# Values' weight slabs in pairs with 512 moving columns, in a kernel of three transformer layers

## The reference

```python
h = _rmsnorm(x, g_mix[layer])
proj = jnp.einsum('bsd,de->bse', h, w_in[layer])
sb_q, sb_k, sb_v, da_q, da_k, da_v = jnp.split(proj, ...)      # 512 columns each
o_a = _stick_breaking_attention(heads(sb_q), heads(sb_k), heads(sb_v))
o_b = _diff_attention(q1, q2, k1, k2, heads(da_v), lam)        # q, k normed and rotated
...
proj = xn @ w_in                                                # second layer
q, k, v = proj[..., :1024], proj[..., 1024:2048], proj[..., 2048:3072]
log_f = jax.nn.log_sigmoid(proj[..., 3072:] + b_f)              # forgetting gates
o = causal_block_attention(q, k, v, 1.0 / math.sqrt(64), jnp.cumsum(log_f, axis=1))
```

## Time and profile before

| | us |
|---|---|
| median of 3 runs | 1010.24 |
| lowest, highest | 1009.67, 1011.06 |
| span of the profiled execution | 1007.6 |
| PE busy | 993.9 (99%) |
| DVE busy | 714.1 (71%) |
| ACT busy | 607.8 (60%) |

### The profile page before, as it was taken

The page is one execution under the profiler, slowest core; times in us unless marked ns, Lnnn a source line. Parts: engine busy times, 40 slices in busy tenths (PEclk is TensorE's granted clock), DMA queues, the critical chain, the costliest instruction groups (busy, mean ns, idle before and its releaser), DMA issues.

```text
span 1007.6 us, 19765 instructions
## 1 busy us (share of the span) xinstructions
PE 993.9 (99%) x7214; PEld 923.4 (92%) x7214; DVE 714.1 (71%) x1360; ACT 607.8 (60%) x1094; POOL 59.6 (6%) x79
## 2 busy tenths in 40 slices
PE   8999999999999999999999999999999999999997
PEld 8999989999999999989999999999989999999996
DVE  4668987776666668666496666668977686666665
ACT  5677785575555556565475555557768675555553
POOL 3011110120000002000020000002200010000000
PEclk9999999999999999999999999999999999999999
DMA  7743445466555554433545556564665456565631
GB/s 292 273 149 110 153 145 187 148 206 190 176 181 186 183 189 159 157 127 127 167 146 188 187 187 187 187 187 127 203 194 191 146 167 188 187 187 187 187 125 43
DMA packets 50904, 174.05 MB, mean 173 GB/s; under 512 B 6304, under 2 KB 8864, under 8 KB 50720
## 3 DMA queue, kind: packets, MB, share of 16 engines
q1 hardware_dynamic: 49664, 172.12, 52.9%
q10 hardware_dynamic: 1184, 1.18, 0.6%
HBM read 169.86 MB, written 1.05 MB: 170 GB/s over the span
## 4 chain that ended last, share of the span: by engine, by line
PE 90%; DVE 5%; ACT 2%; DMA 1%; issue 1%; SPq 0%; DVEq 0%; ACTq 0%
PE bank L426 89%; DVE w_lo L1485 2%; PE bank L647 1%; DVE a_pair L1504 1%; DMA stage<-slab_dram 1%; DVE xT L1515 1%; DVE arena L1478 0%; ACT w_hi L1032 0%; ACT a_pair L1067 0%; DVE soft_s L1566 0%; ACT soft_p L1124 0%; ACT w_hi L1016 0%; DVE tmp L1478 0%; DVE tmp L1712 0%; DVE arena_r L1485 0%
## 5 line engine op out<-in xcount | busy, mean ns | idle before, releaser
L426 PE MATMUL bank<-a_pair,w_hi 128*128 128x256 f32 (+1 forms) x1992 | 537.8, 342 | 2.8 <-DVE w_lo L1485 2.7
L426 PE MATMUL bank<-a_pair,w_lo 128*128 128x256 f32 x1488 | 417.6, 282 | 0.0
L1485 DVE TENSOR_TENSOR w_lo<-stage,w_hi 128x1024 fp32r<-128x1024 f32 (+2 forms) x322 | 387.4, 1211 | 8.4 <-ACT w_hi L1016 3.5
L426 PEld LDWEIGHTS bank<-a_pair,w_hi 128*128 128x128 f32 x1992 | 343.4, 190 | 48.6 <-DVE w_lo L1485 4.0
L426 PE MATMUL bank<-arena_r,w_hi 128*128 128x256 f32 x1792 | 328.8, 284 | 0.4 <-DVE arena_r L1485 0.2
L426 PEld LDWEIGHTS bank<-arena_r,w_hi 128*128 128x128 f32 x1792 | 278.4, 191 | 5.6 <-DVE arena_r L1485 1.4
L426 PEld LDWEIGHTS bank<-a_pair,w_lo 128*128 128x128 f32 x1488 | 283.1, 190 | 0.0
L426 PE MATMUL bank<-arena_r,w_lo 128*128 128x256 f32 x896 | 252.7, 283 | 0.0
L1016 ACT ACTIVATE w_hi<-stage 128x1024 fp32r<-128x1024 f32 x192 | 202.4, 1055 | 33.4 <-PE bank L426 33.4
L1032 ACT ACTIVATE w_hi<-stage 128x1024 fp32r<-128x1024 f32 (+2 forms) x126 | 128.0, 1026 | 79.5 <-PE bank L426 69.7
L426 PEld LDWEIGHTS bank<-arena_r,w_lo 128*128 128x128 f32 x896 | 171.0, 191 | 0.0
(11 more groups left out here) (185 smaller groups left out, 674.8 us busy)
## 6 DMA issues: line engine op xcount, KB each, us to landing
stage<-slab_dram SPq DMA_DIRECT2D x319, 512.0 KB, 4.2
con<-con_dram SPq DMA_DIRECT2D x1, 1153.5 KB, 10.6
xT<-xT_dram SPq DMA_DIRECT2D x4, 256.0 KB, 5.5
arena<-arena ACTq DMA_DIRECT2D x1, 1024.0 KB, 8.9
arena<-tmp SPq DMA_DIRECT2D x32, 32.0 KB, 3.2
out_dram<-arena SPq DMA_DIRECT2D x3, 256.0 KB, 2.4
tmp<-arena SPq DMA_DIRECT2D x16, 16.0 KB
vec<-vec_dram SPq DMA_DIRECT2D x1, 213.5 KB, 11.5
```

The lines of the kernel that those rows point to most:

```text
L426: return nc.tensor.matmul(out, lhsT, rhs, start=start, stop=True, skip_group_check=True)
L1485: return nc.vector.tensor_tensor(out, a, hi.bitcast(f32), ALU.subtract)
```

## The change

Values slabs are multiplied in pairs. The two slabs of a pair hold the same 512 channels and together 512 columns of values; they stand in neighbouring slots, and one matmul moves 2 x 256 columns into a whole PSUM bank. A pair is two products: the first (i even) does token half 0 with both slabs, the second token half 1 with both slabs, in two banks (4 and 5 in the first group, 2 and 3 in the others). Each is 4 channel chunks x 3 matmuls of 512 columns. `slab_done` is raised by two at the end of the second product. PE waits ahead of the first product for the low parts of both slabs.

To bring slabs of a pair together the order of loading and computing changes (`QKV_ORDER`): group SB has its four values slabs at 4 to 7, DA at 8 to 11 (all queries and keys first), FOX at 4 to 7 and 14 to 17. Rounds 5, 6 and 7 of `FOX_AT` move from 17, 21, 23 to 19, 22, 24. `v_out` evicts 512 columns per token half, once per two pairs, and `v_taken` counts to 4 instead of 8. Queries and keys use banks 0 to 3 (4, 0, 1, 3 in round 4), and those that come to banks 2 and 3 after values wait for `v_taken`. The differential attention's norm sums move from bank 3 to bank 4. ACT's loops keep their order, with `v_out(n)` acting in the last turn of two pairs.

The diff, cut to its core:

```diff
+
+QKV_ORDER = {"plain": (0, 1, 2, 3, 4, 10, 5, 11, 6, 7, 8, 9), "diff": (0, 1, 2, 3, 6, 7, 8, 9, 4, 10, 5, 11),
+             "fox0": (0, 2, 1, 3, 4, 10, 5, 11, 6, 8, 7, 9), "fox1": (0, 2, 4, 10, 5, 11, 1, 3, 6, 8, 7, 9)}
-FOX_AT = {FOX + s: k for k, s in enumerate((6, 8, 10, 12, 15, 17, 21, 23))}
+FOX_AT = {FOX + s: k for k, s in enumerate((6, 8, 10, 12, 15, 19, 22, 24))}
-        QK_BANK, V_BANK = (4, 0, 1, 2), 3
+        def v_bank(S, t):
+
+            return bank[(2 if S else 4) + t]
 
         def qk_half(J, c):
 
-            if J > 4 and c == 0:
-                return half(2, 1)
-            return half(QK_BANK[c], 0)
+            return half((4, 0, 1, 3)[c] if J == 4 else c, 0)
+
+        def qkv_role(n):
+
+            first = next(at for at in (FOX + 12, FOX, DA, SB) if n >= at)
+            S, c = (SB, DA, FOX, FOX + 12).index(first), n - first
+            v_at = (4, 8, 4, 2)[S]
+            if v_at <= c < v_at + 4:
+                return "v", S, c - v_at
+            J, c = divmod(c if c < v_at else c - 4, 4)
+            return "qk", 2 * S + J, c
 
         def soft_bank(g):
             if g < HEADS:
...
-            return bank[(1, 0)[side] if j else 3]
+            return bank[(1, 0)[side] if j else 4]
...
-                load(n, n + {1: 1, 2: -1}.get((n - FOX) % 6, 0))
+                load(n, n - (n - FOX) % 12 + QKV_ORDER["fox1" if n >= FOX + 12 else "fox0"][(n - FOX) % 12])
             for n in range(FOXO, FFN2):
...
 
-            def qkv_slab(J, c, n, m):
-
-                slot = n % SLOTS
-                if c < 4:
-                    if J:
-                        pe.wait_ge(qk_taken, 4 * J + c - 3)
-                    first = J in (0, 4) and c == 0
-                    if first and J:
-                        first_column_slabs(n, [half(QK_BANK[i], 0) for i in range(2)], m)
-                    elif first:
-                        very_first_slabs()
-                    elif J not in (0, 4) or c != 1:
-                        column_slab(n, slot, qk_half(J, c))
+            def qkv_slab(n, m):
+
+                kind, J, c = qkv_role(n)
+                if kind == "v":
+                    values_in(J, c, n)
                     return
-                pe.wait_ge(lo_made, n + 1)
-                if J and c == 4:
-                    pe.wait_ge(v_taken, J)
-                if J == 3 and c == 4:
-                    pe.wait_ge(q_factor, 1)
+                if J:
+                    pe.wait_ge(qk_taken, 4 * J + c - 3)
+                if J in (5, 6) and c >= 2:
+                    pe.wait_ge(v_taken, J - 2)
+                if J == 0 and c == 0:
+                    very_first_slabs()
+                elif J == 4 and c == 0:
+                    first_column_slabs(n, [qk_half(J, i) for i in range(2)], m)
+                elif J not in (0, 4) or c != 1:
+                    column_slab(n, n % SLOTS, qk_half(J, c))
+
+            def values_in(S, i, n):
+
+                e, t = divmod(i, 2)
+                if t == 0:
+                    pe.wait_ge(lo_made, n + 2)
+                if e == 0 and S:
+                    pe.wait_ge(qk_taken, (0, 16, 20, 24)[S] + t - 1)
+                slots = slice((n - t) % SLOTS, (n - t) % SLOTS + 2)
                 for k in range(4):
                     w = slice(k * TOK, (k + 1) * TOK)
-                    for t in range(2):
-                        x = (slice(None), 4 * (c - 4) + k, slice(t * P, t * P + P))
-                        last = by_tokens(w_hi[:, slot, w], w_lo[:, slot, w], half(V_BANK, t), a_hi[x], a_lo[x],
-                                         c == 4 and k == 0 and t == 0)
-                last.then_inc(slab_done, 1)
-
+                    x = (slice(None), 4 * e + k, slice(t * P, t * P + P))
+                    last = by_tokens(w_hi[:, slots, w], w_lo[:, slots, w],
+                                     v_bank(S, t).rearrange("p (j n) -> p j n", j=2), a_hi[x], a_lo[x],
+                                     e == 0 and k == 0)
+                if t:
+                    last.then_inc(slab_done, 2)
 
             def sb_scores(c):
...
                 pe.wait_ge(pair_sq, i + 1)
-                if i == 0:
-                    pe.wait_ge(v_taken, 3)
                 if side:
                     mm(pair_bank(side, j)[:, :], con[:, C_PAIR:C_PAIR + P], sq[:, :], True).then_inc(pair_sum, 1)
                     return
...
+                if n == 4:
+                    norm_sum(0)
+                if n == 5:
+                    norm_cols(rB, r_ready, 1, bank[7][:, 256:258], col_done)
+            for n in range(DA, GATE):
+                qkv_slab(n, 0)
+                if n in (DA + 6, DA + 8):
+                    da_norm_sum((n - DA - 6) // 2)
+                attend(n)
             for c in range(16):
                 n = GATE + c
                 if c >= 2:
                     pe.wait_ge(g_taken, c - 1)
+                elif c:
+                    pe.wait_ge(v_taken, 2)
                 else:
-                    pe.wait_ge(qk_taken, 16)
+                    pe.wait_ge(q_factor, 1)
                 column_slab(n, n % SLOTS, half(GATE_BANK[c % 2], 0))
...
             rows_out(FOXO, lambda c: (fo_hi[:, c, :], fo_lo[:, c, :]), lambda c: (o_hi, c + 1),
-                     lambda c: (o_lo, c + 1), free={0: (qk_taken, 32), 6: (v_taken, 8)})
+                     lambda c: (o_lo, c + 1), free={2 * i: (qk_taken, 29 + i) for i in range(4)})
             ffn(1, FFN2)
             for i in range(9):
...
 
-            def v_out(J, v, n):
+            def v_out(n):
+
+                kind, S, i = qkv_role(n)
+                if kind != "v" or i != 3:
+                    return
+                v, at = ((sb_v, 0), (da_v, 0), (fox_v, 0), (fox_v, 512))[S]
                 act.wait_ge(slab_done, n + 1)
-                act.wait_ge(col_ready, 1 if J < 4 else 2)
-                j = J % 2 if J < 4 else J - 4
+                act.wait_ge(col_ready, 1 if S < 2 else 2)
                 for t in range(2):
-                    last = nc.scalar.activation(v[:, t, j * TOK:(j + 1) * TOK], half(V_BANK, t), ACT.Copy,
+                    last = nc.scalar.activation(v[:, t, at:at + 512], v_bank(S, t)[:, :], ACT.Copy,
                                                 scale=r_col[:, t:t + 1])
                 last.then_inc(v_taken, 1)
 
...
                     sb_high(SB_AT[n - 1])
-                if n % 6 == 5:
-                    v_out(n // 6, da_v, n)
+                v_out(n)
                 next_hi(n)
                 attend(n)
             def gates_out(c):
```

More of the change, by code:

```diff
@@ L332, in first_load @@
             def first_load(n):
[L333 removed]
+                sp.dma_start(stage[:, n, :], slab_d[QKV_ORDER["plain"][n]]).then_inc(loaded[n], 16)
             sp.dma_start(vec[:, 0:V_BGATE], vec_d[:, 0:V_BGATE]).then_inc(in_gain, 16)
@@ L471, in very_first_slabs @@
                         pe.wait_ge(alo_ready, k + 1)
-                        last = by_weights(i, k * P, half(QK_BANK[i], 0), a_hi[:, k, :], a_lo[:, k, :], k == 0)
+                        last = by_weights(i, k * P, qk_half(0, i), a_hi[:, k, :], a_lo[:, k, :], k == 0)
                     if ks[-1] == 7:
@@ L815, in _ @@
                 mm(half(7, 0), soft_t[:, 0, 0:P], soft_t[:, 0, 0:TOK], True)
[L816 to L830 removed]
+            for n in range(SB, DA):
+                qkv_slab(n, 0)
[4 more added lines that the diff above has]
+            for n in range(DA, GATE):
+                qkv_slab(n, 0)
+                if n in (DA + 6, DA + 8):
+                    da_norm_sum((n - DA - 6) // 2)
+                attend(n)
             for c in range(16):
@@ new lines, in _ @@
+            for n in range(FOX, FOXO):
+                qkv_slab(n, 2)
+                if n == FOX + 1:
+                    pe.wait_ge(wf_ready, 1)
+                    for k in range(NC):
+                        mm(bank[7][0:32, TOK:2 * TOK], wf_split[:, k, :], a_hi[:, k, :], k == 0)
+                        last = mm(bank[7][0:32, TOK:2 * TOK], wf_split[:, k, :], a_lo[:, k, :], False)
+                    last.then_inc(f_raw, 1)
+                if n == FOX + 2:
+                    norm_sum(2)
+                if n == FOX + 3:
+                    norm_cols(rB, r_ready, 3, bank[7][:, 0:2], col_done)
+                if n == FOX + 4:
+                    pe.wait_ge(f_turned, 1)
+                    for t in range(2):
+                        last = nc.tensor.transpose(bank[7][:, 32 * t:32 * t + 32],
+                                                   tmp[0:32, 0, t * P:(t + 1) * P], ident[0:32, 0:32])
+                    last.then_inc(f_done, 1)
+                if n == FOX + 5:
+                    pe.wait_ge(f_ready, 1)
+                    for r in (0, 64):
+                        out = bank[7][r:r + 16, 256:512]
+                        mm(bank[7][r:r + 16, 128:256], forget[:, 64:80], con[:, C_TRIF:C_TRIF + P], True)
+                        mm(out, forget[:, 64:80], con[:, C_TRIF:C_TRIF + TOK], True)
```

(17 more changed lines are left out.)

65 lines of the change are left out of this document (11 added, 54 removed).

## The result

The changed kernel takes 1023.86 us (median of 4 runs, 1021.04 to 1024.81); the kernel before, beside it, 1010.33 us. The ratio is 1.0135, with a 95% interval of 1.0122 to 1.0147: 13.5 us slower. The forecast was 1023.9, range 1017 to 1028.

The account below looks back on a forecast made before the run. PE, busy 99% of the span, was taken as the bound. Waits of 14.4 us, less 1.9 for matmuls and 0.3 taken back, plus 1.5 for the clock, made 13.7 and a time of 1023.9 us; range 1017 to 1028.

Parts of the forecast that it names:

- first projections: At the start, PE waits for DVE's low parts of slabs 5 and 7: 0.3 and 0.6, together 0.9 us.
- masks: Stick-breaking round 2: ACT's cast waits for the pair's end, then exponentials and POOL's masks follow; PE waits 3.6 us.
- gates: Forgetting gates, turn FOX+5: exp and ln stand behind a cast released only at the pair's end; PE waits 1.9 us.
- first softmax: Pair FOX+6, 7: exponentials and probabilities follow a cast waiting for the pair's end; PE waits 2.9 us before transposing.
- copies: Pairs FOX+14 to 17, rounds 3 and 4: ACT's copy of transposed probabilities stands behind a cast; PE waits 1.6 us twice.
- The clock: PE's clock falls to half rate after the longer of two new waits exceeding 2.68 us, counted once: 1.5 us lost.
- 0.3 taken back in the gates: PE's existing 1.80 us wait for DVE in the gates shrinks by 0.3, lowering the net cost from 12.5 to 12.2.
- The wider matmuls: Eight pairs of values slabs, 24 matmuls of 512 columns instead of 48 of 256 each: 1.9 us gained.
- 2.6 us around the span: Difference between the profiled span, 1007.6 us, and the runs' median, 1010.24, taken as untouched by the change.
- Case (a): Rival: clock lost at both long waits and 512 columns cost as much as twice 256; 1027.3 us, chance 0.16.
- (b): Rival: gates' 1.80 us wait vanishes, masks shortest, clock never lost, copies at lower bound; 1019.3 us, or 1017; chance 0.14.
- (c): Rival: ACT reaches its attention steps before the pair's end, so the old cover holds; 1009.2 or 1008.3 us, chance 0.05.

Follow-up runs that it names:

- The first run: Changed kernel with no ACT cast in the turn of a pair's first slab and both casts in its second's; 1012.39 us, ratio to before 1.0026.
- the runs with 256 columns: Changed kernel's order, slabs multiplied singly with 256 columns: signalled singly 1019.21 us; signalled by pairs 1030.57; singly, second group's values in banks 0 and 1, 1011.81.
- filled and unfilled kernel: Filled: changed kernel with matmuls whose result nobody uses in all five long PE waits, 1022.05 us; unfilled: the changed kernel itself, 1023.86.
- the recovered version: Changed kernel with ACT's casts in the pair's second turn, and slab places, banks and ACT steps moved to remove the waits left; 1008.85 us, ratio 0.9996.
- recovered, 256 columns: 512-column pairs with ACT's casts moved and remaining waits removed, but each 512-column matmul replaced by two of 256; 1010.21 us, ratio 1.0008.

## Why the prediction was right

**The mechanism** is what it said: ACT's order around the pair's single signal. The first run shows it (11.5 of 13.5), and the runs with 256 columns show that neither order nor width does it. Place by place, predicted and measured: first projections 0.9 and 0.80; masks 3.6 and 2.42; squares 0.5 and 0.47; gates 1.9 and 1.75; first softmax 2.9 and 2.81; copies 1.6 and 1.6 and 1.57 and 1.62; eviction 0.8 and 0.59; scores 0.6 and 0.52. Sum 14.4 and 12.55.

**The number** came out to 0.04 us, which its terms did not deserve; several were mis-sized and cancel:

- *The masks*, 1.2 too long. The term is "masks done 2.5 us after these start", from the pair of masks that took 1.99. Here the exponentials took 0.85 and the masks 0.79, less than the shortest of the trace before, and 2.8 was given as a floor.
- *The clock*, 1.5 once. The profiled execution lost 3.2; filled and unfilled kernel differ by 0.5 to 1.8 in the median. So once fits a median, but by luck, since the reason given, the length of the longer wait, is not what decides (below).
- *0.3 taken back in the gates*: nothing was. The 1.80 of the earlier trace rows is 1.80 after, and 1.79 or 1.80 in every profile here. I take it that DVE's late step there depends on PE's own scores a few slabs earlier, so that the whole chain moved along; no run tested it.
- *The wider matmuls*, 1.9: 2.2 by rows, 1.4 by medians.
- *Left out*: PE's restart behind each wait, some 1.0 in all (the estimate above), and 0.8 in the latent stage, where the same wait lies between 0.61 and 1.39 in ten of the eleven profiles.
- *2.6 us around the span* is 1.7 and an execution that was 0.9 faster than its median.

**The rivals.** Case (a) was right on the clock for the profiled execution, which lost it behind both long waits, and wrong on the width: 512 columns gained 0.14 a product. Part given back (b) had one thing right, the shorter masks, and its absorbed 1.80 wrong. The faster case (c) wanted ACT to come to its steps before the pair's end; the first and the recovered run built just that, and its 1008.3 to 1009.2 is where the recovered version came out, at 1008.85. And the prediction did not see the bank that comes free 0.05 us ahead of the second product; it had nothing to say on what the new order of banks costs.

## What to carry to other kernels

A signal that covers two units of work is late for the first of them, and everything in program order behind the wait for it is late too; look for what stands behind that wait on the in-order engine, not for who reads the signal. When two units are joined, move the consumers' first-unit work behind their second-unit wait in the same edit: here six moved casts were worth 11 us, and the joined matmuls 1.4 to 2.2. Before an order of banks is changed, find each bank's last reader in the trace and by how much it is early.

## What the hardware did that was not expected

**The clock after a wait is not a function of its length.** The same 2.4 and 2.8 us of idle PE that halved the clock in the changed kernel left it alone in the run with the pairs' signal and 256 columns:

```profile
94.25 0.87 PE L439 MATMUL bank<-soft_t,arena 128*64 128x256 f32 x8 [2.43 <-issue]
...
432.71 0.55 PE L663 MATMUL bank<-con,soft_p 128*128 128x128 f32 x3 [2.81 <-DVE soft_p L1646]
```
```profile
95.00:96.00 1.00, 1.00 (x12) 0.79 (x9) 0.42 (x1) 0.40 (x2) 0.00 (x0) 1.00 0.00 0
...
434.00:435.00 1.00, 1.00 (x10) 1.00 (x10) 1.00 (x3) 1.00 (x3) 0.00 (x0) 1.00 0.29 53
```

The unchanged wait of 1.80 us in the gates was followed by 1.2 GHz in one profile (recovered, 256 columns) and by 2.4 GHz in the ten others. The one:

```profile
134.00:135.00 1.00, 1.00 (x7) 1.00 (x6) 0.96 (x4) 1.00 (x2) 0.00 (x0) 0.50 0.00 0
```

In the profile with all five waits filled there was no fall between the start and the tail. What else decides was not settled; in this kernel a wait of 1.6 to 2.8 us is best priced with 0 to 1.7 us on top.

**POOL's masks and DVE's low parts take turns.** The same two masks of 128 x 256 of the first round, and DVE beside them, in the recovered version (first fence) and in the changed kernel (second):

```profile
55.90 1.22 DVE L1523 TENSOR_TENSOR w_lo<-stage,w_hi 128x1024 fp32r<-128x1024 f32 x1
57.03 0.41 DVE L1516 TENSOR_TENSOR arena<-bank,rB 128x256 f32<-128x256 f32 x1
57.37 1.21 DVE L1523 TENSOR_TENSOR w_lo<-stage,w_hi 128x1024 fp32r<-128x1024 f32 x1
...
56.27 2.58 POOL L2118 TENSOR_SCALAR_AFFINE_SELECT soft_t<-soft_t 128x256 f32<-128x256 f32 x2 [31.46 <-ACT soft_t L1143]
```
```profile
56.32 1.21 DVE L1499 TENSOR_TENSOR w_lo<-stage,w_hi 128x1024 fp32r<-128x1024 f32 x1
57.45 0.42 DVE L1492 TENSOR_TENSOR arena<-bank,rB 128x256 f32<-128x256 f32 x1
57.78 1.45 DVE L1499 TENSOR_TENSOR w_lo<-stage,w_hi 128x1024 fp32r<-128x1024 f32 x1
...
57.00 1.15 POOL L2094 TENSOR_SCALAR_AFFINE_SELECT soft_t<-soft_t 128x256 f32<-128x256 f32 x2 [32.02 <-ACT soft_t L1130]
```

With DVE idle (84.4 to 88.4 in the changed kernel) the two masks took 0.79, some 0.4 each; over all eleven profiles, eleven masks met no DVE instruction, and each of them took 0.40 or 0.41. In the first fence they read as one mask in the gap at 57.1, between two low parts, and one behind the second low part, at 58.5: 2.58 in all. In the second both fit around the gap at 57.5, and it is the low part that comes out longer, 1.45 for 1.22. The Trainium skill, "SBUF — State Buffer", section "Terms", says that VectorE and GpSimd share a pair of ports under a lock, held for a whole instruction. These rows agree with it, though no run here varied DVE's work alone; that a scaling out of PSUM lets POOL in is read from where the masks fall, not tested. So a mask's price is set by where it falls in DVE's row: 0.79 to 2.58 in these traces, which is why the prediction's masks were too long. In the recovered version PE came for the first masks at 58.51 (59.21 in the kernel before) and waited 0.48 for them.
